# First attention of a two-layer mixer: how the side work of PE is dealt over the steps

## The chip, the cores and the metric

The kernel is one program on 1 core of a Trainium2 chip. The metric is the device time of that core in microseconds (us). TensorE is called PE, VectorE DVE, ScalarE ACT, GpSimd POOL, and SP issues most of the DMAs. All arithmetic is in float32; large products are made of three matmuls on operands that are split in a high and a low part.

## The reference

The program is a chain of blocks on a sequence of 512 tokens of width 1024. The change touches the attention of the first block, which runs in each of its two layers:

```python
h = rmsnorm(x, ln1_g[i]) @ w_in[i]
(fq, fk, fv, ff, dq, dk, dv, c_q, c_kv, k_r) = jnp.split(h, split_points, axis=-1)
o_fox  = fox_group(fq, fk, fv, ff, fgate_b[i])           # 4 heads of 64, causal, forget-gate bias
o_diff = diff_group(dq, dk, dv, ..., lam_init)           # 4 heads: softmax 1 - lam * softmax 2, values of 128, norm
o_mla  = mla_group(c_q, c_kv, k_r, ..., w_uq, w_ukv)     # 4 heads: q, k, v from a latent of 256 and of 128, with rope
x = x + jnp.concatenate([o_fox, o_diff, o_mla], axis=-1) @ w_o[i]
up = causal_dwconv(rmsnorm(x, ln2_g[i]) @ w_up[i], conv_w[i], conv_b[i])
x = x + (jax.nn.silu(up[..., :D_FF]) * up[..., D_FF:]) @ w_down[i]
```

Every softmax runs over the keys up to the query's own block of 128 (`fox_group` is causal inside it, the others use a mask of chunks of 64). After the two layers come an mLSTM mixer and a windowed attention, which the change leaves alone.

## The kernel before, in words

Activations lie transposed, a feature tile of 128 on the partitions and the 512 tokens along the free dimension. The attention of a layer is one loop over steps `s` = 0 to 67, written out on PE, ACT and DVE alike. Units 0 to 63 are the score blocks of 128 queries: `unit1(u)` gives the kind, the query block `i` and the head. Units 0 to 15 are the first group, in pairs of heads (n = 0, 1), units 16 to 47 the second (n = 2 to 5), of which an even and the following odd unit share one output, and units 48 to 63 the latent one. A unit of query block `i` has 128 x (i + 1) keys, so the work of a step grows with `i`, which is 0 to 3 over each eight steps.

In step `s` PE computes the scores of unit `s` (L762, L765) into bank `s % 3`, transposes the weights of unit `s - 3` (L778), multiplies those of unit `s - 4` with the values (`chain`, L593), and then does its filling, `fill1(s)`. DVE adds the bias and takes the maximum of the scores (L2074), mixes the two softmaxes of the second group (L2083, L2085, L2088), copies every other transposed block (L2103), scales the output (L2112) and then does `follow1(s)`. ACT computes the exponential (L1442), copies the other transposed blocks (L1451), and then does its own `follow1(s)`, which ends with splitting a weight unit into its high part (L1224), if `splits` names one for the step; POOL makes the low part (L2582). Between the splits POOL has the `scale_diff` operations (L2617), whose order is written out. Split weights have three slots: a unit can be split only when PE is through with the unit three back, and a load by SP waits for the split five units back.

The filling is the work that the softmax does not need at once:

- `tile_part`: K tiles ("k") and Q tiles ("q") of the next pairs of heads. A piece ("k", k0, kn) is kn of the 8 parts of the sum, three matmuls of 512 columns each (L563). Behind a whole K tile ACT writes its high half by 4 operations (L1323) and DVE its low half by 4 (L2002); behind a Q tile 2 and 2 (L1319, L1997). `LOW_STEPS` says in which step DVE does the low half.
- `value_tile`: one of four value tiles of 24 matmuls of 256 columns (L563), copied out by ACT.
- in steps 37 to 45 the latent parts: "mv" (values) and "mk" (keys), which ACT alone copies out (L1390, L1406), and "mq" (queries), of which ACT copies a part (L1401) and DVE turns the rest by three operations (L2041, L2043, L2047); and `turn_out`, which transposes the finished outputs of two heads (L685). ACT (L1366, L1369) and DVE (L2017, L2020) split these into `hH` and `hLo`.
- `out_part`: a piece of the output product with `w_o` (L563), which DVE adds to `x` (L2027); 12 matmuls in part 0, 6 in parts 1 and 2.

All filling uses banks 6 and 7 of the eight. Before PE writes a bank, `claim` makes it wait for the engine that reads the last result in it. Behind the last score, in step 64 and after the loop, the last outputs are transposed and part 2 follows.

## Time and profile before

| | us |
|---|---|
| median of 3 runs | 2560.44 (2558.16 to 2563.48) |
| the profiled execution | 2555.06 |
| its span in the profile | 2553.0 |
| PE busy | 2472.5 |
| DVE busy | 1222.8 |
| ACT busy | 987.8 |
| POOL busy | 978.5 |

A profile row of the timeline gives the start in us from the span's start, the duration in us, the engine, the line, the operation, what it writes and reads, how many instructions of that kind were merged, and in brackets how long the engine had been idle before it and whom it waited for. A matmul is pipelined: its duration is its latency, and the distance between two starts is what it costs. A step begins with the row of L762 in bank `s % 3`. In the first layer step 0 starts at 73.01 us, in the second at 735.27 us.

### The profile page before, as it was taken

The page shows a single profiled execution, that of the slowest core. Times are in us where ns is not written, and L with a number is a line of the kernel's source. Part 1 is how long each engine was busy: PE and PEld are TensorE (multiplying, and loading weights), DVE is VectorE, ACT ScalarE, POOL GpSimd, SP SyncE. Part 2 cuts the span into 40 slices and gives each one's busy share as a digit, 9 for nine tenths or more (in the row PEclk, how much of TensorE's full clock was granted, in tenths as well). Part 3 has the DMA queues.
Part 4 walks back from the last instruction along what each step waited for, and adds up shares of the span by engine and source line. Part 5 has one row for each costly group of instructions (what it writes and reads, how often), then busy time and mean ns, then how long its engine had stood idle before and what let it go on. Part 6 is the DMA issues. An engine that isn't in the chain of part 4 may idle for free.

```text
span 2553.0 us, 32345 instructions
## 1 busy us (share of the span) xinstructions
PE 2472.5 (97%) x12450; PEld 2013.9 (79%) x12450; DVE 1222.8 (48%) x2205; ACT 987.8 (39%) x1731; POOL 978.5 (38%) x512
## 2 busy tenths in 40 slices
PE   9998999999999899999999999999999999899998
PEld 6886788888788678888888778778787778887766
DVE  4356589530235747984116431622251252556663
ACT  5455344432345635444333313131222322455552
POOL 3322356764432225567663223222222323322231
PEclk9999999999999999999999999999999999999999
DMA  4211245322321114532331111112111111111000
GB/s 176 74 46 62 95 157 190 99 95 97 114 75 54 47 65 147 192 131 95 114 110 66 50 42 53 56 33 66 58 56 35 50 58 42 55 65 31 29 25 34
DMA packets 54584, 200.48 MB, mean 79 GB/s; under 512 B 6176, under 2 KB 6176, under 8 KB 53664
## 3 DMA queue, kind: packets, MB, share of 16 engines
q1 hardware_dynamic: 52272, 189.27, 21.9%
q10 hardware_dynamic: 2160, 9.15, 1.0%
q8 instruction: 100, 1.64, 0.3%
q14 instruction: 52, 0.43, 0.1%
HBM read 196.29 MB, written 2.10 MB: 78 GB/s over the span
## 4 chain that ended last, share of the span: by engine, by line
PE 77%; DVE 15%; ACT 3%; issue 2%; POOL 2%; DVEq 0%; ACTq 0%; POOLq 0%
PE ps L871 25%; PE ps L543 18%; PE ps L563 16%; PE ps L593 10%; DVE arena L1938 7%; DVE arena L2131 1%; PE ps L762 1%; DVE arena L2128 1%; DVE norm_sq L1902 1%; PE ps L1184 1%; POOL norm_acc L2595 1%; POOL wl L2582 1%; PE ps L778 1%; DVE hl L1914 1%; PE ps L988 1%
## 5 line engine op out<-in xcount | busy, mean ns | idle before, releaser
L2582 POOL TENSOR_TENSOR wl<-wring,wh 128x1024 fp32r<-128x1024 f32 (+1 forms) x305 | 770.5, 2526 | 1245.7 <-ACT wh L1224 1234.2
L1224 ACT ACTIVATE wh<-wring 128x1024 fp32r<-128x1024 f32 (+1 forms) x305 | 317.2, 1043 | 544.3 <-PE ps L871 307.9
L543 PE MATMUL ps<-hh,wh 128*128 128x512 f32 x768 | 300.0, 391 | 10.0 <-DVE hl L1914 5.1
L543 PE MATMUL ps<-hh,wl 128*128 128x512 f32 x768 | 299.0, 389 | 0.0
L543 PE MATMUL ps<-hl,wh 128*128 128x512 f32 x768 | 298.9, 389 | 0.0
L593 PE MATMUL ps<-arena 128*128 128x512 f32 (+2 forms) x912 | 265.2, 427 | 15.8 <-ACT arena L1451 5.8
L593 PEld LDWEIGHTS ps<-arena 128*128 128x128 f32 x912 | 141.5, 191 | 101.0 <-issue 77.4
L563 PE MATMUL ps<-hh,wh 128*128 128x512 f32 (+1 forms) x472 | 202.4, 429 | 5.0 <-DVE hl L2563 2.4
L563 PE MATMUL ps<-hh,wl 128*128 128x512 f32 (+1 forms) x472 | 189.1, 401 | 0.0
L563 PE MATMUL ps<-hl,wh 128*128 128x512 f32 (+1 forms) x472 | 188.7, 400 | 0.0
L1938 DVE CUSTOM_DVE_ANT_0 arena<-arena 128x1024 f32<-128x1024 f32 x96 | 182.6, 1902 | 8.6 <-DVE arena L2131 0.3
L543 PEld LDWEIGHTS ps<-hh,wh 128*128 128x128 f32 x768 | 144.1, 188 | 44.6 <-DVE hl L1914 5.2
L543 PEld LDWEIGHTS ps<-hh,wl 128*128 128x128 f32 x768 | 144.1, 188 | 30.1
L543 PEld LDWEIGHTS ps<-hl,wh 128*128 128x128 f32 x768 | 144.2, 188 | 28.7
L871 PE MATMUL ps<-hh,wh 128*128 128x512 f32 x368 | 144.3, 392 | 0.0
L871 PE MATMUL ps<-hl,wh 128*128 128x512 f32 x368 | 144.3, 392 | 0.0
L871 PE MATMUL ps<-hh,wl 128*128 128x512 f32 x368 | 143.1, 389 | 0.0
L543 PE MATMUL ps<-gu_h,wh 128*128 128x512 f32 x352 | 137.1, 390 | 0.0
L543 PE MATMUL ps<-gu_h,wl 128*128 128x512 f32 x352 | 136.9, 389 | 0.0
L543 PE MATMUL ps<-gu_l,wh 128*128 128x512 f32 x352 | 136.9, 389 | 0.0
L1442 ACT ACTIVATE arena<-arena,st 128x128 f32<-128x128 f32 (+3 forms) x128 | 71.8, 561 | 155.0 <-DVE st L2074 154.2
L2074 DVE CUSTOM_DVE_ANT_0 arena<-ps,arena 128x128 f32<-128x128 f32 (+3 forms) x128 | 62.5, 488 | 122.7 <-PE ps L765 63.8
(342 smaller groups left out, 5229.8 us busy)
## 6 DMA issues: line engine op xcount, KB each, us to landing
wring<-wts SPq DMA_DIRECT2D x290, 512.0 KB, 3.3
arena<-wts SPq DMA_DIRECT2D x48, 512.0 KB, 4.1
wring<-wts SPq DMA_DIRECT2D x16, 384.0 KB, 3.0
xL<-xt SPq DMA_DIRECT2D x4, 512.0 KB, 5.5
arena<-tab SPq DMA_DIRECT2D x1, 2048.0 KB, 16.0
arena<-cv ACTq DMA_DIRECT2D x2, 1024.0 KB, 4.9
arena<-tab ACTq DMA_DIRECT2D x1, 2048.0 KB, 7.8
out_t<-xL ACTq DMA_DIRECT2D x8, 256.0 KB, 2.0
```

The costliest lines, as they stand in the source:

```text
L543: mm = nc.tensor.matmul(o[0], a, b, start=start and k == first and j == 0, stop=stop and k == last and j == 2)
L563: mm = nc.tensor.matmul(dst, a, b, start=start and x == 0 and i == 0 and j == 0, stop=stop and x == len(us) - 1 and i == kn - 1 and j == 2)
L593: last = nc.tensor.matmul(dst, a, b, start=start and i == 0, stop=stop and i == len(pairs) - 1)
L762: last = nc.tensor.matmul(ps[:, s % 3, 0:ke], a, b, start=x == 0, stop=x == len(bs) - 1 and kind != "fox")
L778: last = nc.tensor.transpose(ps[:, 3 + tb, 128 * j:128 * j + 128], sbuf[:, u % 4, 128 * j:128 * j + 128], idn)
L871: mm = nc.tensor.matmul(dst, a, b, start=x == 0 and i == 0 and j == 0, stop=x == len(us) - 1 and i == kn - 1 and j == 2)
L988: nc.tensor.matmul(c, mlv[:, s, cols], cut(dense(s, 0), TC), start=s == 0, stop=s == 1)
L1224: nc.scalar.activation(wh[:, sn % SPLIT_SLOTS, :kn * w], raw(u)[:, :kn * w], ACT.Copy).then_inc(act_done, tick("act", ("hi", u)))
L1442: nc.scalar.activation(sbuf[:, s % 4, 0:ke], sbuf[:, s % 4, 0:ke], ACT.Exp, scale=-1.0, bias=mx1[:, s % 16:s % 16 + 1], accum_out=rs1[:, s ...
L1938: V.tensor_tensor_reduce(out=ada_dump, in0=raw(u), in1=crow[:, j, :], scale=1.0, scalar=0.0, op0=ALU.mult, op1=ALU.add, accum_out=modv[:, ...
L2074: V.tensor_tensor_reduce(out=sbuf[:, s % 4, 0:ke], in0=ps[:, s % 3, 0:ke], in1=bias, scale=-scale, scalar=3e38, op0=ALU.add, op1=ALU.min, ...
L2582: G.tensor_tensor(wl[:, sn % SPLIT_SLOTS, :kn * w], raw(u)[:, :kn * w], wh[:, sn % SPLIT_SLOTS, :kn * w].bitcast(F32), ALU.subtract).then_inc(
```

## The change

The filling of steps 0 to 31 is dealt evenly. A piece now has the number of its tile as well, (x, n, k0, kn); a value tile can be done in parts; two K tiles and two Q tiles come first in each 16 steps, and the value tiles come last, where they stood between the first and the second K tile before. The order of the weight units, of the splits on ACT and POOL and of `LOW_STEPS` follows. Steps 32 to 36 keep their pieces as `LAST_PIECES`.

In steps 37 to 47 the latent parts and the transposed outputs alternate: "mv" in steps 37 and 39, "mk" in 37, 39, 41 and 43, `turn_out` in 38 and 40, "mq" in 41, 42, 44 and 46. The first piece of output part 0 moves from step 46 to 45. Pieces 6 and 7 of output part 1 move from steps 61 and 62 to steps 64 and 65, into banks 2 and 1, ahead of the `turn_out` of step 64. `fill1` and `follow1` therefore run in every step up to 67.

```diff
-            if n in (0, 1, 3):
-                add(("v", l, (n + 1) // 2), "w_in", l, 0, KT, [((FV, DV, DV + 256)[(n + 1) // 2], 256)])
+            if n in (0, 2, 4):
+                add(("v", l, n // 2), "w_in", l, 0, KT, [((FV, DV, DV + 256)[n // 2], 256)])
+        add(("ukv", l), "w_ukv", l, 0, 1, [(128 * h, 64) for h in range(4)] + [(128 * h + 64, 64) for h in range(4)])
         add(("uq", l), "w_uq", l, 0, 2, [c for h in range(4)
                                          for c in ((96 * h, 96), (96 * h + 80, 16), (96 * h + 64, 16))])
-        add(("ukv", l), "w_ukv", l, 0, 1, [(128 * h, 64) for h in range(4)] + [(128 * h + 64, 64) for h in range(4)])
...
-PIECES = [[("k", 0, 3)], [("k", 3, 3)], [("k", 6, 2), ("q", 0, 1)], [("q", 1, 4)], [("q", 5, 3)],
-          [("v", 0, 0)], [("v", 1, 0)], [("v", 2, 0)], [("v", 3, 0)],
-          [("k", 0, 3)], [("k", 3, 3)], [("k", 6, 2), ("q", 0, 1)], [("q", 1, 3)], [("q", 4, 2)], [("q", 6, 2)], []]
-LOW_STEPS = {3: ("k", 1), 5: ("q", 1), 12: ("k", 2), 14: ("q", 2), 19: ("k", 3), 21: ("q", 3), 28: ("k", 4),
-             30: ("q", 4), 35: ("k", 5), 36: ("q", 5)}
-OUT0_STEPS = (46, 47, 48, 49, 50, 51, 52, 54)
+PIECES = [[("k", 1, 0, 3)], [("k", 1, 3, 3)], [("k", 1, 6, 2), ("q", 1, 0, 1)], [("q", 1, 1, 3)], [("q", 1, 4, 3)],
+          [("q", 1, 7, 1), ("k", 2, 0, 2)], [("k", 2, 2, 3)], [("k", 2, 5, 3)], [("q", 2, 0, 3)], [("q", 2, 3, 3)],
+          [("q", 2, 6, 2), ("v", 0, 0, 2)], [("v", 0, 2, 6)], [("v", 1, 0, 6)], [("v", 1, 6, 2), ("v", 2, 0, 4)],
+          [("v", 2, 4, 4), ("v", 3, 0, 2)], [("v", 3, 2, 6)]]
+LAST_PIECES = [[("k", 1, 0, 3)], [("k", 1, 3, 3)], [("k", 1, 6, 2), ("q", 1, 0, 1)], [("q", 1, 1, 4)], [("q", 1, 5, 3)]]
+LOW_STEPS = {3: ("k", 1), 6: ("q", 1), 8: ("k", 2), 11: ("q", 2), 19: ("k", 3), 22: ("q", 3), 24: ("k", 4),
+             27: ("q", 4), 35: ("k", 5), 36: ("q", 5)}
+MV_STEPS = {37: 0, 39: 1}
+MK_STEPS = {37: 2, 39: 3, 41: 0, 43: 1}
+MK_BANKS = {2: 7, 3: 7, 0: 7, 1: 6}
+MQ_STEPS = {41: 0, 42: 1, 44: 2, 46: 3}
+MQ_BANKS = (6, 7, 6, 6)
+OT_STEPS = {38: (0, 1), 40: (2, 3), 53: (4, 5)}
+OUT0_STEPS = {45: (0, 7), 47: (1, 7), 48: (2, 6), 49: (3, 7), 50: (4, 6), 51: (5, 7), 52: (6, 6), 54: (7, 6)}
+OUT1_STEPS = {55: (0, 7), 56: (1, 6), 57: (2, 7), 58: (3, 6), 59: (4, 7), 60: (5, 6), 64: (6, 2), 65: (7, 1)}
+
+
+def pieces_of(s):
+
+    return PIECES[s % 16] if s < 32 else LAST_PIECES[s - 32] if s < 37 else ()
...
-                def value_tile(j, t, b):
+                def value_tile(j, t, b, k0=0, kn=KT):
 
                     us = views(("v", l, j))
-                    claim([b], "act", "v", l, j, t)
-                    product(ps[:, b, 0:256], lat_toks(t), us, ("v", l, j, t),
-                            *([("used", x[0]) for x in us] if t == NT - 1 else []))
+                    if k0 == 0:
+                        claim([b], "act", "v", l, j, t)
+                    part = []
+                    for u, o, n, v in us:
+                        x, y = max(o, k0), min(o + n, k0 + kn)
+                        if x < y:
+                            part.append((u, x, y - x, [r[:, x - o:y - o, :] for r in v]))
+                    end = k0 + kn == KT
+                    product(ps[:, b, 0:256], lat_toks(t), part, *([("v", l, j, t)] if end else []),
+                            *([("used", x[0]) for x in us] if end and t == NT - 1 else []), start=k0 == 0, stop=end)
...
-                    pieces = PIECES[s % 16] if s < 32 else PIECES[s - 32] if s < 37 else ()
-                    for x, c, m in pieces:
+                    for x, n, c, m in pieces_of(s):
                         if x == "v":
-                            value_tile(1 + s // 16, c, 6 + c % 2)
+                            value_tile(1 + s // 16, n, 6 + n % 2, c, m)
                         else:
-                            tile_part(x, 2 * (s // 16) + (1 if s % 16 < 9 else 2), 6 if x == "k" else 7, c, m)
-                    if s == 37:
-                        pe.wait_ge(dve_done, at("dve", "h", ("ckv", l), 0))
+                            tile_part(x, 2 * (s // 16) + n, 6 if x == "k" else 7, c, m)
+                    if s in MV_STEPS:
+                        x = MV_STEPS[s]
+                        if x == 0:
+                            pe.wait_ge(dve_done, at("dve", "h", ("ckv", l), 0))
                         (n, _, w), = plain(("ukv", l))
-                        for t in range(NT):
-                            if t % 2 == 0:
-                                claim([6 + t // 2], "act", "mv", l, t // 2)
-                            chain(ps[:, 6 + t // 2, 256 * (t % 2):256 * (t % 2) + 256],
+                        claim([6], "act", "mv", l, x)
+                        for t in (2 * x, 2 * x + 1):
+                            chain(ps[:, 6, 256 * (t % 2):256 * (t % 2) + 256],
                                   [(cn[:, 2, 128 * t:128 * t + 128], w[:, 0, 256:512])], ("mv", l, t))
-                    elif s in (38, 39):
-                        for x in range(2):
-                            turn_out(2 * (s - 38) + x, 6 + x, 0, 1, 2, 3)
-                    elif 40 <= s < 44:
-                        r = s - 40
+                    if s in OT_STEPS:
+                        for x, k in enumerate(OT_STEPS[s]):
+                            turn_out(k, 6 + x, 0, 1, 2, 3)
+                    if s in MQ_STEPS:
+                        r = MQ_STEPS[s]
+                        b = MQ_BANKS[r]
                         if r == 0:
                             for m in range(2):
                                 pe.wait_ge(dve_done, at("dve", "h", ("cq", l), m))
                         (n, _, w), = plain(("uq", l))
-                        claim([7 - r % 2], "dve", "mq", l, r)
-                        chain(ps[:, 7 - r % 2, :], [(w[:, k, 128 * r:128 * r + 128], cn[:, k, :]) for k in range(2)],
+                        claim([b], "dve", "mq", l, r)
+                        chain(ps[:, b, :], [(w[:, k, 128 * r:128 * r + 128], cn[:, k, :]) for k in range(2)],
                               ("mq", l, r), *([("used", n)] if r == 3 else []))
-                    elif s in (44, 45):
+                    if s in MK_STEPS:
+                        h = MK_STEPS[s]
+                        b = MK_BANKS[h]
                         (n, _, w), = plain(("ukv", l))
-                        for h in (2 * s - 88, 2 * s - 87):
-                            claim([7 - h % 2], "act", "mk", l, h)
-                            chain(ps[0:64, 7 - h % 2, :], [(w[:, 0, 64 * h:64 * h + 64], cn[:, 2, :])], ("mk", l, h),
-                                  *([("used", n)] if h == 3 else []))
-                    elif s in OUT0_STEPS:
-                        out_part(0, OUT0_STEPS.index(s), 6 + s % 2)
-                    elif s == 53:
-                        for x in range(2):
-                            turn_out(4 + x, 6 + x, 0, 1, 2, 3)
-                    elif 55 <= s < 63:
+                        claim([b], "act", "mk", l, h)
+                        chain(ps[0:64, b, :], [(w[:, 0, 64 * h:64 * h + 64], cn[:, 2, :])], ("mk", l, h),
+                              *([("used", n)] if h == 1 else []))
+                    if s in OUT0_STEPS:
+                        out_part(0, *OUT0_STEPS[s])
+                    if s in OUT1_STEPS:
                         if s == 55:
                             pe.wait_ge(dve_done, at("dve", "ot", l, 5, 1))
-                        out_part(1, s - 55, 6 + s % 2)
+                        out_part(1, *OUT1_STEPS[s])
...
-                splits = {0: ("q", l, 1), 1: ("v", l, 1, first), 3: ("v", l, 1, second), 5: ("k", l, 2),
-                          9: ("q", l, 2), 10: ("k", l, 3), 12: ("q", l, 3), 15: ("v", l, 2, first),
-                          19: ("v", l, 2, second), 21: ("k", l, 4), 25: ("q", l, 4), 26: ("k", l, 5),
-                          28: ("q", l, 5), 31: ("wo", l, 0, 0), 35: ("wo", l, 0, 1), 37: ("wo", l, 0, 2),
-                          48: ("wo", l, 0, 3), 50: ("wo", l, 1, 0), 52: ("wo", l, 1, 1), 55: ("wo", l, 2, 0),
-                          59: ("wo", l, 2, 1)}
+                splits = {0: ("q", l, 1), 1: ("k", l, 2), 4: ("q", l, 2), 6: ("v", l, 1, first), 9: ("v", l, 1, second),
+                          12: ("k", l, 3), 16: ("q", l, 3), 17: ("k", l, 4), 20: ("q", l, 4), 22: ("v", l, 2, first),
+                          25: ("v", l, 2, second), 28: ("k", l, 5), 32: ("q", l, 5), 33: ("wo", l, 0, 0),
+                          35: ("wo", l, 0, 1), 37: ("wo", l, 0, 2), 48: ("wo", l, 0, 3), 50: ("wo", l, 1, 0),
+                          52: ("wo", l, 1, 1), 55: ("wo", l, 2, 0), 59: ("wo", l, 2, 1)}
...
-                    if s < nu:
-                        follow1(s)
-                    elif s == nu:
+                    follow1(s)
+                    if s == nu:
                         low_out(6, 6, 0, 1, 2)
                         low_out(7, 7, 0, 1, 2)
...
-                split(("k", l, 1))
-                split(("q", l, 1))
-                split(("v", l, 1))
-                for n in (2, 3):
+                for n in (1, 2):
                     split(("k", l, n))
                     split(("q", l, n))
+                split(("v", l, 1))
+                split(("k", l, 3))
+                split(("q", l, 3))
+                split(("k", l, 4))
+                split(("q", l, 4))
                 split(("v", l, 2))
-                split(("k", l, 4))
                 scale_diff(0)
-                split(("q", l, 4))
+                scale_diff(1)
                 split(("k", l, 5))
-                scale_diff(1)
+                scale_diff(2)
                 split(("q", l, 5))
-                scale_diff(2)
                 split(("wo", l, 0, 0))
```

The other two engines' `follow1` read the same tables: ACT and DVE do their part of each piece in the step in which PE does it, apart from `LOW_STEPS`.

## Rows read from the trace of the kernel before

**Rows 1.** The page: busy us of each engine.

```profile
PE 2472.5 (97%) x12450; PEld 2013.9 (79%) x12450; DVE 1222.8 (48%) x2205; ACT 987.8 (39%) x1731; POOL 978.5 (38%) x512
```

**Rows 2.** Stretches, layer 1: us; busy of PE, PEld, DVE, ACT, POOL; PEclk; DMA; GB/s.

```profile
73.00:125.95 52.95, 51.59 (x339) 46.84 (x337) 21.07 (x72) 27.31 (x60) 16.75 (x7) 1.00 0.22 70
125.95:131.90 5.95, 5.19 (x21) 4.19 (x22) 1.97 (x9) 2.63 (x6) 2.38 (x1) 0.71 0.03 5
131.90:175.23 43.33, 43.33 (x278) 38.91 (x276) 25.71 (x76) 24.17 (x61) 12.32 (x7) 1.00 0.17 55
175.23:183.24 8.01, 5.60 (x21) 4.23 (x20) 5.83 (x15) 5.54 (x16) 1.74 (x3) 0.79 0.20 65
...
195.38:229.94 34.56, 26.84 (x115) 16.03 (x114) 26.18 (x69) 19.80 (x52) 7.13 (x6) 1.00 0.12 38
...
280.56:291.73 11.17, 8.56 (x66) 7.21 (x64) 5.60 (x18) 3.68 (x9) 0.00 (x0) 1.00 0.01 1
291.73:303.00 11.27, 11.27 (x43) 9.18 (x44) 4.15 (x6) 5.00 (x8) 7.13 (x5) 0.85 0.68 234
```

**Rows 3.** The same stretch of steps 37 to 46 in the second layer.

```profile
857.62:892.18 34.56, 26.85 (x115) 16.04 (x114) 26.19 (x69) 19.79 (x52) 7.14 (x6) 1.00 0.12 38
```

**Rows 4.** PE's waits, 73 to 292 us: total, times, longest.

```profile
PE ps L762 <- DVE qs L1997: 3.2, 2, 1.8
PE ps L593 <- ACT arena L1451: 2.9, 3, 1.5
...
PE ps L593 <- DVE arena L2103: 1.4, 1, 1.4
```

**Rows 5.** PE's timeline: matmuls of the filling, 512 and 256 columns.

```profile
74.22 0.39 PE L563 MATMUL ps<-hh,wl 128*128 128x512 f32 x1
74.45 0.40 PE L563 MATMUL ps<-hh,wh 128*128 128x512 f32 x1
...
88.42 0.28 PE L563 MATMUL ps<-wh,hl 128*128 128x256 f32 x1
88.54 0.28 PE L563 MATMUL ps<-wh,hh 128*128 128x256 f32 x1
```

**Rows 6.** Stretches: steps 14 and 17.

```profile
120.32:123.05 2.73, 2.73 (x18) 2.39 (x16) 1.61 (x9) 1.80 (x5) 1.05 (x1) 1.00 0.24 35
131.90:135.28 3.38, 3.38 (x23) 2.99 (x21) 1.35 (x5) 0.49 (x2) 0.00 (x0) 1.00 0.46 151
```

**Rows 7.** PE's timeline: starts of steps 16 and 32, filling of step 16.

```profile
125.95 0.33 PE L762 MATMUL ps<-kh,qs 128*128 128x128 f32 x1 [1.34 <-DVE qs L1997]
...
129.54 0.63 PE L563 MATMUL ps<-hh,wh 128*128 128x512 f32 x1
...
178.97 0.33 PE L762 MATMUL ps<-kh,qs 128*128 128x128 f32 x1 [1.82 <-DVE qs L1997]
```

**Rows 8.** Instructions of L2085; timelines of DVE and POOL, step 36; page, L1224.

```profile
L2085 DVE SCALAR_TENSOR_TENSOR st<-st x32: 219/219/1981, 136.3 to 897.0; 128x1 f32<-128x1 f32 x32
...
194.50 1.97 DVE L2085 SCALAR_TENSOR_TENSOR st<-st 128x1 f32<-128x1 f32 x1
...
194.08 2.38 POOL L2582 TENSOR_TENSOR wl<-wring,wh 128x1024 fp32r<-128x1024 f32 x1 [0.34 <-ACT wh L1224]
...
L1224 ACT ACTIVATE wh<-wring 128x1024 fp32r<-128x1024 f32 (+1 forms) x305 | 317.2, 1043 | 544.3 <-PE ps L871 307.9
```

**Rows 9.** Timelines of PE and DVE, steps 40 to 43.

```profile
208.49 1.95 PE L593 MATMUL ps<-arena,wring 128*128 128x512 f32 x4 [2.38 <-DVE hl L2017]
...
217.22 1.16 PE L593 MATMUL ps<-arena 128*128 128x128 f32 x8 [1.55 <-ACT arena L1451]
...
210.48 0.70 DVE L2041 TENSOR_TENSOR arena<-ps,arena 32x512 f32<-32x512 f32 x1 [0.29 <-PE ps L593]
```

**Rows 10.** Steps 61 and 62 as a stretch; PE's timeline behind the last score.

```profile
sum 6.50, PE 6.50 PEld 4.92 DVE 3.86 ACT 2.01 POOL 0.00; mean PE 3.25 PEld 2.46 DVE 1.93 ACT 1.00 POOL 0.00
...
291.73 0.52 PE L563 MATMUL ps<-hh,wh 128*128 128x512 f32 x1 [0.76 <-DVE hl L2020]
```

More of the change, by code:

```diff
@@ new lines, in follow1 @@
+                def follow1(s):
+                    for x, n, c, m in pieces_of(s):
+                        if c + m == KT:
+                            if x == "v":
+                                evacuate_v(1 + s // 16, n, 6 + n % 2)
+                            else:
+                                high_tile(x, 2 * (s // 16) + n, 6 if x == "k" else 7)
+                    if s in MV_STEPS:
+                        x = MV_STEPS[s]
+                        act.wait_ge(pe_done, at("pe", "pv", l, 31))
+                        act.wait_ge(pe_done, at("pe", "mv", l, 2 * x + 1))
+                        nc.scalar.activation(mv[:, 2 * x:2 * x + 2, :],
+                                             ps[:, 6, :].rearrange("p (t c) -> p t c", t=2), ACT.Copy).then_inc(
+                            act_done, tick("act", ("mv", l, x)))
+                    if s in OT_STEPS:
+                        for x, k in enumerate(OT_STEPS[s]):
+                            high_out(k, 6 + x, 0, 1, 2, 3)
+                    if s in MQ_STEPS:
+                        r = MQ_STEPS[s]
@@ L2034, in follow1 @@
                         low_tile(x, n, 6 if x == "k" else 7)
-                    if 40 <= s < 44:
-                        r = s - 40
-                        b = 7 - r % 2
+                    if s in OT_STEPS:
+                        for x, k in enumerate(OT_STEPS[s]):
+                            low_out(k, 6 + x, 0, 1, 2, 3)
+                    if s in MQ_STEPS:
+                        r = MQ_STEPS[s]
+                        b = MQ_BANKS[r]
                         dve.wait_ge(pe_done, at("pe", "mq", l, r))
@@ L2048, in follow1 @@
                             dve_done, tick("dve", ("mq", l, r)))
-                    elif s in (38, 39):
-                        for x in range(2):
-                            low_out(2 * (s - 38) + x, 6 + x, 0, 1, 2, 3)
-                    elif s in OUT0_STEPS:
-                        add_out(0, OUT0_STEPS.index(s), 6 + s % 2)
-                    elif s == 53:
-                        for x in range(2):
-                            low_out(4 + x, 6 + x, 0, 1, 2, 3)
-                    elif 55 <= s < 63:
-                        add_out(1, s - 55, 6 + s % 2)
+                    if s in OUT0_STEPS:
+                        add_out(0, *OUT0_STEPS[s])
+                    if s in OUT1_STEPS:
+                        add_out(1, *OUT1_STEPS[s])
                 nu = 64
```

37 lines of the change are left out of this document (8 added, 29 removed).

## The prediction

> **What bounds the kernel now.** I read the engine totals first. PE is busy 2472.5 us of a span of 2553.0 us, every other engine under half of it [rows 1], and the change removes no matmul. So the only time to be won is time in which PE waits, or runs at the lower of its two clocks. Next I cut the first attention of the first layer into stretches at the starts of its score matmuls. In a "waited" stretch PE's busy time falls short of the stretch; in a "slow" one the granted clock falls under 1.00 [rows 2]. PE idles 1.36 (to 125.95) + 0.76 + 2.41 + 7.72 + 2.61 = 14.9 us in the five that have any to speak of. The clock is 1.2 instead of 2.4 GHz in three places: 0.71 over 5.95 us, 0.79 over 8.01 us and 0.85 over 11.27 us. Work lost there is (1 - 0.71) x 5.95 = 1.73, 0.21 x 8.01 = 1.68 and 0.15 x 11.27 = 1.69 us. The second layer repeats the longest of them to 0.01 us [rows 3], so I work out one layer and double it. The two layers hold 2 x (14.9 + 5.1) = 40 us: this is the ceiling.
>
> Then the list of waits tells who ends the idle times: L1997 (the low half of a query tile) 3.2 us, L1451 (ScalarE's copy of transposed weights) 2.9 us, L2103 (VectorE's copy) 1.4 us [rows 4]; L2017 (the low half of a transposed output) ends 2.38 us at once [rows 9].
>
> **Part 1: the filling dealt evenly over 16 steps.** The unit prices come from successive starts: a 512-column matmul of the filling takes 0.23 us, a 256-column one 0.12 us [rows 5]. Before, steps 0 to 15 held 9, 9, 9, 12, 9 matmuls of 0.23 us, then four value tiles of 24 x 0.12 = 2.88 us, then 9, 9, 9, 9, 6, 6 and nothing. The sum is 96 x 0.23 + 96 x 0.12 = 33.6 us; the new list has the same matmuls, 9 x 0.23 = 2.07 us or 18 x 0.12 = 2.16 us in each step. PE's work is unchanged.
>
> What goes are two waits per layer. Step 15 has no filling and step 16 needs the query tile finished at step 14: the row at 125.95 says that PE idled 1.34 us for L1997. Then the clock fell, the filling's matmuls took 0.63 us instead of 0.40 (129.54) [rows 7], and step 16 took 5.95 us [rows 2]. Step 17, the same shape and filling, took 3.38 [rows 6]. The excess is 2.57 us, and with the 1.34 us before it 3.9 us. The same happens at step 32: 1.82 us idle ahead of it [rows 7], 2.41 in all, and 1.68 us of clock: 4.1 us. In the new order the query tile of pair 2 is complete in step 10 and its low half runs in step 11, five steps before its reader; that of pair 4 runs in step 27. What ends last in step 15 is then a value tile, whose first reader comes in step 20. I take both waits and both drops of the clock as gone: 3.9 + 4.1 = 8.0 us, less 0.5 us for small waits that the steps with K tiles may show. The bounds are 8.0 and 4.6 us (the waits go, 1.34 + 0.76 + 2.41, but the clock falls somewhere else).
>
> Costs of this part. Each value tile is now cut in two, with no more matmuls and no more signals. In steps 5 to 8 the filling falls from 2.88 to 2.07 us; whether the softmax chain is then late can be read from step 14, which has the longest keys (512) and only 1.38 us of filling: PE was busy all its 2.73 us [rows 6]. So 0, up to 13 us (a rival below). The ring of three split weights is next: both units of a value tile are freed only by the last piece, in steps 15 and 31. Then ScalarE's split (1.04 us) in step 16 and GpSimd's 2.38 us [rows 8] have to be done before step 18's third piece, about 7.7 us later (2 x 2.9 + 1.9). With a softmax exponential (0.6 us on average) and the start of the step ahead of it on ScalarE the tile is ready after some 4.7 us. That leaves 3 us of slack: 0. SP's loads go in the new order of the units; a load waits for the split five units back, which is steps old, and `ukv` and `uq` only swap: 0. Part 1 gives 7.5 us a layer.
>
> **A resource to weigh.** L2085 on VectorE, 0.22 us in the median, took 1.97 us from 194.50, while GpSimd ran a 2.38 us split from 194.08, and ended with it [rows 8]. The copy L2103 behind it then ended PE's 1.42 us wait in step 37. Splits issued by ScalarE in odd steps meet this operation in the next even step. The operation runs in steps 18 to 48 only. Before there were six such splits (19, 21, 25, 31, 35, 37), now there are five (17, 25, 33, 35, 37). So this costs nothing new, and the 1.42 us in step 37 stays, since step 35's split stays. (The Trainium skill, "SBUF — State Buffer", section "Who interferes with whom", says that a VectorE instruction with two SBUF inputs and a GpSimd one that reads SBUF exclude each other for the whole instruction; this trace agrees, 1.97 against 0.22 us. If the stalls landed on a full VectorE they would cost 2 us each by it; it alone would not turn the sign.)
>
> **Part 2: steps 37 to 47.** Before, PE idled 7.72 us from 195.38 to 229.94 with VectorE busy 26.18 us of 34.56 [rows 2]. The order held all value parts, then four transposed outputs, then the latent queries one a step, then the keys. The largest wait, 2.38 us at 208.49, has the first query part waiting for the low halves of outputs 2 and 3 (L2017), whose banks it reuses; 1.55 us at 217.22 come from VectorE and ScalarE being late, as VectorE works through three query operations of 0.7 us in each of four steps [rows 9]. Now key and value parts, which only ScalarE reads, lie between the outputs, and the queries stand in 41, 42, 44 and 46. I followed the new order through the three engines with these durations. Step 37: 1.42 stays. Step 39: 0.8 for L1451 stays, 0.5 for the low half of output 0 stays (it now holds up the value part). Step 40: 0.3. Step 41: 0.5 for a copy by VectorE, and 1.2 for the low half of output 2, the old 2.38 us halved: it still comes some 2.9 us behind its transposes, as ScalarE has the norm of step 39 and an exponential first, but 1.7 us of scores and value products of step 41 now lie between. Step 43: 0.1. Step 44: 0.65, since the third query part takes the bank of key part 1, whose copy stands behind a softmax exponential. Sum 5.5 against 7.7: 2.2 us, of which I take 1.7. The bounds are 0 (every wait finds a successor, as VectorE has the same work in the same stretch) and 6.3 (all but the 1.42 go).
>
> **Part 3: two output pieces behind the last score.** Pieces 6 and 7 of output part 1, 6 x 0.23 = 1.38 us each, leave steps 61 and 62 and stand behind the value products of steps 64 and 65. Steps 61 and 62 took 3.25 us each with a piece, so 1.87 without. So everything from the last score on comes 2.76 us earlier. VectorE was busy 3.86 us in two such steps with the additions of two pieces, 0.69 us each, which leaves (3.86 - 1.38) / 2 = 1.24 us of work in a step of 1.87 [rows 10] and the chain keeps pace. From the start of step 63 to the last part PE waited 2.61 us [rows 2], in five waits of 0.24, 0.53, 0.54, 0.54 and, before the last part, 0.76 us [rows 10]. Piece 6 delays the transposes of outputs 6 and 7 by 1.38 us, and with them the low halves (L2020) that stood ahead of the copy for step 66: the 0.53 us wait goes, the last three waits stay, as product, scaling, transposing, splitting and the first matmul of the last part wait for each other whatever stands before. Piece 7 takes the place of 0.5 us of waiting and moves the rest by 0.9. In sum 1.4 us of 2.76 is hidden (bounds 0 and 2.6).
> The third fall of the clock, 1.69 us, comes with the last part's first matmuls, from 291.73 [rows 2]. The thin stretch ahead of it, the 7 us up to 291.73, shrinks to the last 4.2 us, as piece 7 has full matmuls. I count half of it, 0.8 us, between 0 and 1.7.
>
> **Sum.** One layer 7.5 + 1.7 + 1.4 + 0.8 = 11.4 us, two 23 us. The profiled execution took 2555.06 us (the span 2553.0 and 2.06 around it), so it would take 2532. It lies 5.4 us under the median of 2560.44; from the median I predict 2537.5.
>
> **Rivals.**
> A, the clock follows the waits: steps 38 and 40 hold only transposes beside the softmax, so from step 40 to the first query part in 41 PE has some 4.7 us of thin work with 2 us of waiting in it, about what stood before each fall. Against it: 195.38 to 229.94 has clock 1.00 with 7.72 us idle [rows 2]. One fall there and one left in the tail give back 2 x (1.7 + 0.8), and part 2 at nothing 2 x 1.7 more: 2537.5 + 8.4 = 2546. (The Trainium skill, "TensorE: Matmul & The Clock Gate", section "A second HAM failure mode: psum-queue depth-cycling", says that frequent small idle times between groups of matmuls make the clock oscillate. That would put a fall already in the old steps 37 to 47; the trace has none there.) Chance 0.22.
> B, the long-key steps miss their filling: four steps of each 16 with 2.88 - 2.07 = 0.81 us less cover, all waited for, 0.81 x 4 x 2 x 2 = 13 us: 2550. Against it is step 14. Chance 0.08.
> C, slower: the key and query tiles now land in steps 7, 8 and 10, 11, beside the longest softmax, and VectorE, which has 4 x 0.7 us for a key tile and 2 x 0.7 for a query tile (the size of L2041, [rows 9]) in one lump ahead of the next step's softmax, sends PE waiting for each. Eight tiles a layer are 4 x 2.8 + 4 x 1.4 = 17 us, two layers 34, against 23 gained: 2560.4 + 11 = 2571. It decides once such a lump is longer than the two steps (5 us and more) by which PE runs ahead. Against it: VectorE was busy 25.71 us of 43.33 in steps 17 to 30 [rows 2]. Chance 0.04.
> D, the change does more: nearly all waits of part 2 go too, and the third clock fall with them: 23 + 2 x (4.6 + 0.9) = 34: 2526. Chance 0.14.
> E, it does nothing, as another wait or the ring of weights takes each one's place: 2560. Chance 0.04. The forecast itself holds 0.48.
>
> **Range.** The forecast's own range is 2531 to 2544. With A, most of B, and half of D: 2527 to 2551. Faster than before by over 0.2% (5 us; what a measurement here can tell from no change) are the forecast, A, B, D: 0.92; same 0.04; slower 0.04.
>
> **What would show it.** No idle time ahead of steps 16 and 32 and clock 1.00 there; steps 16 and 32 near 3.4 and 2.7 us; the first query part (step 41) waiting about 1 us for L2017's successor in place of 2.38; steps 37 to 46, which hold the same parts in both orders, near 32.9 us instead of 34.56; from the start of step 63 to the last part's first matmul 12.5 us instead of 11.17, since step 63 starts 2.8 us earlier. The prediction is wrong if PE waits in steps 5 to 12, if the clock falls between steps 38 and 43, or if the weight ring's split ends a wait in step 18 or 34.

## The result, and the profile after

The changed kernel took 2538.09 us in the median of 4 runs (2534.49 to 2539.47), beside 2559.3 us for the kernel before. The ratio is 0.9917, with an interval of 0.9902 to 0.9932. So it is faster, by 21 us, and 0.6 us off the forecast of 2537.5. Timed again later beside its own runs of the kernel before, it took 2538.33 us (2534.25 to 2540.8), with a ratio of 0.991 [0.9893, 0.9926] (experiment 9).

The profiled execution took 2534.49 us. Its page starts like this, to be read against [rows 1]:

```profile
span 2532.8 us, 32353 instructions
...
PE 2466.3 (97%) x12450; PEld 2009.7 (79%) x12450; DVE 1217.8 (48%) x2205; ACT 986.0 (39%) x1731; POOL 977.3 (39%) x512
```

The number of matmuls is the same. PE is busy 6 us less, most of it the clock (5 us, see below), and idle 14 us less: (2553.0 - 2472.5) - (2532.8 - 2466.3) = 14.0 us.

The same cut into stretches as in [rows 2], of the first layer. The columns are window, length, busy time and count of PE, PEld, DVE, ACT and POOL, granted clock, DMA share and GB/s. The rows are step 0 to 15, step 16, steps 17 to 30, steps 31 and 32, steps 37 to 46, step 63 to the last part, and the last part's first 11 us:

```profile
73.08:124.78 51.70, 51.67 (x339) 46.89 (x338) 22.31 (x76) 26.54 (x60) 14.35 (x6) 1.00 0.19 62
124.78:128.05 3.27, 3.27 (x22) 2.90 (x21) 0.66 (x4) 2.20 (x5) 0.66 (x1) 1.00 0.02 5
128.05:169.60 41.55, 41.22 (x259) 36.75 (x258) 25.33 (x81) 25.78 (x64) 14.93 (x8) 1.00 0.20 66
169.60:175.28 5.68, 5.68 (x40) 5.21 (x39) 2.84 (x10) 3.01 (x12) 0.43 (x1) 1.00 0.10 36
187.43:219.42 31.99, 26.54 (x116) 15.86 (x114) 23.80 (x66) 18.55 (x49) 6.68 (x6) 1.00 0.05 17
267.68:281.01 13.33, 11.25 (x78) 9.50 (x78) 6.60 (x21) 4.86 (x12) 0.00 (x0) 1.00 0.00 1
281.01:292.30 11.29, 11.29 (x51) 9.35 (x52) 4.88 (x8) 5.17 (x8) 8.69 (x5) 1.00 0.69 234
```

PE's busy time equals the length in step 16 and in steps 31 and 32: both waits of part 1 are gone, and the clock is 1.00 where it was 0.71 and 0.79. One wait of 0.33 us is new, in step 21, in both layers; it is the only one over 0.05 us in steps 0 to 36:

```profile
141.69 0.49 PE L607 MATMUL ps<-arena 128*128 128x128 f32 x2 [0.33 <-DVE arena L2115]
```

In steps 37 to 46 PE still idles 5.4 us, where it idled 7.7. These are the waits, in PE's timeline:

```profile
189.38 0.49 PE L607 MATMUL ps<-arena 128*128 128x128 f32 x2 [1.44 <-DVE arena L2115]
190.91 1.04 PE L607 MATMUL ps<-arena,wring 128*64 128x512 f32 x2 [0.18 <-DVE qs L2012]
195.17 0.71 PE L607 MATMUL ps<-arena 128*128 128x128 f32 x4 [0.79 <-ACT arena L1466]
196.47 1.10 PE L607 MATMUL ps<-wring,arena 128*128 128x256 f32 x4 [0.59 <-DVE hl L2035]
200.97 0.94 PE L607 MATMUL ps<-arena 128*128 128x128 f32 x6 [0.63 <-DVE arena L2115]
202.73 2.96 PE L607 MATMUL ps<-arena,wring 128*128 128x512 f32 x6 [0.82 <-DVE hl L2032]
212.31 1.95 PE L607 MATMUL ps<-arena,wring 128*128 128x512 f32 x4 [0.99 <-ACT arena L1424]
```

Behind the last score, to be read against [rows 10]; the L577 rows from 271.38 are piece 6, those from 274.75 are piece 7:

```profile
270.49 1.08 PE L607 MATMUL ps<-arena 128*128 128x64 f32 x8 [0.24 <-DVE st L2108]
271.38 0.48 PE L577 MATMUL ps<-hh,wh 128*128 128x512 f32 x1
...
273.94 1.00 PE L607 MATMUL ps<-arena 128*128 128x64 f32 x8
274.75 0.48 PE L577 MATMUL ps<-hh,wh 128*128 128x512 f32 x1
...
276.66 1.00 PE L607 MATMUL ps<-arena 128*128 128x64 f32 x8
278.20 1.08 PE L607 MATMUL ps<-arena 128*128 128x64 f32 x8 [0.54 <-DVE arena L2124]
279.82 0.43 PE L706 MATMUL ps<-prmt,arena 128*128 128x128 f32 x2 [0.54 <-DVE arena L2124]
281.01 0.51 PE L577 MATMUL ps<-hh,wh 128*128 128x512 f32 x1 [0.76 <-DVE hl L2035]
```

Of the five waits, only the second (0.53 us) is gone. In the kernel before it was this one:

```profile
287.31 1.08 PE L593 MATMUL ps<-arena 128*128 128x64 f32 x8 [0.53 <-DVE st L2096]
```

Where the 20.2 us between the two spans went, start to start of score matmuls, layer 1 (layer 2 agrees to 0.06 us or better):

| steps | before | after | gain | of it not clock |
|---|---|---|---|---|
| 0 to 36 | 122.37 | 114.35 | 8.02 | 4.6 |
| 37 to 47 | 38.20 | 36.06 | 2.14 | 2.14 |
| 48 to 60 | 40.48 | 40.52 | 0 | 0 |
| 61 to the last part | 17.67 | 17.00 | 0.67 | 0.67 |

What is not clock, 2 x (4.6 + 2.14 + 0.67) = 14.8 us, I count as waits; PE's idle time fell by 14.0 us. What is left, 5.4 us, is clock. The granted clock agrees: before, up to the last part of layer 2, it was low for 3.41 us at six places, 20.5 us in all, and after for 3.4 + 6.8 = 10.2 us; half of the difference is 5.1 us. It is less than the 2 x (3.4 + 1.7) us that the three old places had cost, since the clock now fell in a new place, in the projections at the head of layer 2:

```profile
683.00:695.00 12.00, 11.14 (x42) 9.07 (x43) 0.69 (x1) 1.25 (x2) 6.75 (x4) 0.86 0.41 132
703.00:713.00 10.00, 10.00 (x23) 5.68 (x23) 4.17 (x6) 7.27 (x12) 3.54 (x3) 0.66 0.17 52
```

Layer 2's step 0 therefore started only 735.27 - 727.63 = 7.6 us earlier, though layer 1 had gained 8.02 + 2.14 + 0.67 and the 1.7 us of its last part, 12.5 in all.

### The profile page after: what moved, and what is told of

Read it like the earlier page. It is cut to its first block, busy times and chain, and to the rows that moved or that the text cites. A ratio compares the mean times of both kernels' runs of the same rounds, so it can differ in the third digit from the quotient of the medians.

```text
span 2532.8 us, 32353 instructions
## 1 busy us (share of the span) xinstructions
PE 2466.3 (97%) x12450; PEld 2009.7 (79%) x12450; DVE 1217.8 (48%) x2205; ACT 986.0 (39%) x1731; POOL 977.3 (39%) x512
## 4 chain that ended last, share of the span: by engine, by line
PE 78%; DVE 15%; ACT 3%; issue 2%; POOL 2%; DVEq 0%; ACTq 0%; POOLq 0%
PE ps L890 25%; PE ps L557 19%; PE ps L577 16%; PE ps L607 11%; DVE arena L1953 7%; PE ps L782 2%; DVE arena L2142 1%; DVE arena L2139 1%; DVE norm_sq L1917 1%; PE ps L1203 1%; PE ps L798 1%; POOL norm_acc L2606 1%; POOL wl L2593 1%; DVE hl L1929 1%; PE ps L1007 1%
## 5 line engine op out<-in xcount | busy, mean ns | idle before, releaser
L577 PE MATMUL ps<-hh,wh 128*128 128x512 f32 (+1 forms) x472 | 199.3, 422 | 5.0 <-DVE hl L2574 2.4
L577 PE MATMUL ps<-hh,wl 128*128 128x512 f32 (+1 forms) x472 | 186.6, 395 | 0.0
L577 PE MATMUL ps<-hl,wh 128*128 128x512 f32 (+1 forms) x472 | 185.9, 394 | 0.0
```

The source lines that it names most:

```text
L577: mm = nc.tensor.matmul(dst, a, b, start=start and x == 0 and i == 0 and j == 0, stop=stop and x == len(us) - 1 and i == kn - 1 and j == 2)
```

## The experiments

One table for the stretches, layer 1 / layer 2 where they differ by over 0.1 us; ratios stand with each experiment. Experiments 5 and 9 are those of "after" to 0.13 us; of 6, 7 and 8 the text names the one stretch that each changes.

| kernel | median | steps 0 to 36 | 37 to 47 | 61 to the last part |
|---|---|---|---|---|
| before | 2559 to 2562 | 122.37 | 38.20 | 17.67 |
| after | 2538.09 | 114.35 | 36.06 | 17.00 |
| 1: part 1 alone | 2547.63 | 114.35 | 39.52 / 39.70 | 17.85 / 18.66 |
| 2: parts 1 and 2 | 2541.66 | 114.38 | 36.09 | 17.87 / 18.69 |
| 3: part 3 alone | 2558.32 | 120.78 / 122.36 | 38.21 | 17.00 |
| 4: new order, old lumps | 2541.42 | 115.92 | 36.08 | 17.00 |
| 10: 6, 7 and 8 together | 2529.31 | 114.30 | 34.34 | 16.43 |

**1. Part 1 alone.** The kernel before with the new `PIECES`, `LAST_PIECES`, `LOW_STEPS`, the value tile in parts, and the new orders of units and splits; everything from step 37 on, and `ukv` behind `uq`, as before.

> Only part 1 of the change: the filling of steps 0 to 31 dealt evenly, steps 37 on as before. My theory (the low half of a query tile finished one step before its reader, and the clock that falls behind it) expects steps 0 to 36 of each layer to take 114.4 us as in the changed kernel instead of 122.4, so 16 us less, and the stretch of steps 37 to 46 at its old 34.56 us. The fall of the clock behind the last score (1.7 us a layer) should still be there, as the thin stretch ahead of it is the old one. So about 2543 us. The rival, that the clock behind the last score depends only on how its look falls on the stretch, expects it to be gone in one or both layers here too, 3.4 us less.

Measured: 2547.63 us (2546.3 to 2552.84) against 2560.71, ratio 0.9957 [0.9941, 0.9974]. Steps 0 to 36 have the full gain, 8.0 us in each layer. But in the profiled execution (span 2550.8), the slowest of the four, most of it is given back: the clock fell for 6.8 us in the head of each layer, then in steps 40 and 41 in both layers, and for 6.8 instead of 3.4 us behind the last score. It fell so by 0.014 of the span in sum, against 0.009 before. In the old steps 37 to 47 that costs 1.3 to 1.5 us; the fall, at 205.1 us, comes right behind the old wait of the first query part:

```profile
204.35 3.03 PE L600 MATMUL ps<-arena,wring 128*128 128x512 f32 x4 [2.38 <-DVE hl L2029]
...
203.00:210.00 7.00, 5.64 (x16) 3.25 (x16) 5.47 (x15) 2.71 (x11) 3.08 (x3) 0.76 0.00 1
285.00:295.00 10.00, 8.22 (x31) 6.42 (x31) 2.45 (x6) 2.07 (x4) 2.37 (x1) 0.66 0.49 159
```

Part 1 saves 16 us in its own steps; alone it is worth 13 in the medians (2547.63 us, where 2543 was expected). (A clock that falls and rises again is what the Trainium skill, "TensorE: Matmul & The Clock Gate", section "A second HAM failure mode: psum-queue depth-cycling", gives as the result of frequent short idle times between groups of matmuls. The prediction said that the trace of before has no such fall in steps 37 to 47; this run of the same steps does, in both layers, so the rule holds there in some executions.)

**2. Parts 1 and 2, without part 3.**

```diff
-              ... 60: (5, 6), 64: (6, 2), 65: (7, 1)}
+              ... 60: (5, 6), 61: (6, 7), 62: (7, 6)}
```

> Parts 1 and 2 without part 3: pieces 6 and 7 stand in steps 61 and 62 again. I expect steps 37 to 47 at 36.1 us (38.2 before), and from the start of step 61 to the first matmul of the last part 17.67 us (17.00 in the changed kernel), so 1.3 us more than the changed kernel in both layers. If part 3 is what removed the fall of the clock there, it comes back: another 3.4 us. About 2543 us with it, 2539 us without.

Measured: 2541.66 us (2537.23 to 2542.78), ratio 0.9927 [0.9911, 0.9942]. Steps 37 to 47 are those of the changed kernel to 0.03 us, without a fall in the stretch where experiment 1 has one. Behind the last score the clock fell for 6.8 us in both layers:

```profile
203.00:210.00 7.00, 5.53 (x28) 3.18 (x27) 4.96 (x14) 4.53 (x15) 2.63 (x3) 1.00 0.00 1
282.00:292.00 10.00, 8.23 (x30) 6.33 (x30) 2.46 (x6) 2.38 (x5) 2.37 (x1) 0.66 0.52 170
```

So part 2 is worth 2.1 us of waits a layer, and against the one profile of experiment 1 another 1.4 of clock.

**3. Part 3 alone**, on the kernel before: pieces 6 and 7 of output part 1 in steps 64 and 65, nothing else.

> Only part 3 on the kernel before: pieces 6 and 7 behind the last score. The clock theory (the full matmuls of piece 7 shorten the thin stretch) expects the fall behind the last score gone in both layers and 0.67 us a layer besides: 4.7 us less than before. The rival (the position of the look decides, and nothing moves ahead of that place in layer 1 of the kernel before) expects a fall in at least one of the two layers: 1.3 to 3 us less.

Measured, in 10 runs: 2558.32 us (2555.36 to 2563.37), ratio 0.9995 [0.9984, 1.0005]: nothing that can be told from zero. The stretch is 17.00 us as in the changed kernel, so the gain is 0.67 us a layer and does not depend on the other parts. The clock fell at the last part in layer 1 and not in layer 2, as the rival had it; the 4.7 us of the clock theory lie outside the interval. And step 16 of layer 1, the same instructions as in [rows 2] with the same wait before it, ran at full clock here:

```profile
126.00:132.00 6.00, 4.05 (x25) 3.45 (x26) 3.16 (x12) 2.64 (x6) 2.25 (x1) 1.00 0.01 3
290.00:296.00 6.00, 5.29 (x16) 4.19 (x17) 1.81 (x4) 1.88 (x4) 2.37 (x1) 0.72 0.71 238
952.00:958.00 6.00, 4.15 (x23) 3.34 (x22) 1.75 (x5) 1.50 (x4) 1.92 (x1) 1.00 0.23 64
```

**4. The order or the even sizes?** The changed kernel with its new order of tiles, but the old sizes of the pieces: whole value tiles, and nothing in steps 15 and 31.

```diff
-PIECES = [[("k", 1, 0, 3)], [("k", 1, 3, 3)], [("k", 1, 6, 2), ("q", 1, 0, 1)], [("q", 1, 1, 3)], [("q", 1, 4, 3)],
-          [("q", 1, 7, 1), ("k", 2, 0, 2)], [("k", 2, 2, 3)], [("k", 2, 5, 3)], [("q", 2, 0, 3)], [("q", 2, 3, 3)],
-          [("q", 2, 6, 2), ("v", 0, 0, 2)], [("v", 0, 2, 6)], [("v", 1, 0, 6)], [("v", 1, 6, 2), ("v", 2, 0, 4)],
-          [("v", 2, 4, 4), ("v", 3, 0, 2)], [("v", 3, 2, 6)]]
+PIECES = [[("k", 1, 0, 3)], [("k", 1, 3, 3)], [("k", 1, 6, 2), ("q", 1, 0, 1)], [("q", 1, 1, 4)], [("q", 1, 5, 3)],
+          [("k", 2, 0, 3)], [("k", 2, 3, 3)], [("k", 2, 6, 2), ("q", 2, 0, 1)], [("q", 2, 1, 3)], [("q", 2, 4, 2)],
+          [("q", 2, 6, 2)], [("v", 0, 0, 8)], [("v", 1, 0, 8)], [("v", 2, 0, 8)], [("v", 3, 0, 8)], []]
```

> The changed kernel with the new order (two K and two Q tiles, then the values) but the old sizes: 9, 9, 9, 12, 9, 9, 9, 9, 9, 6, 6 matmuls of 512 columns, four whole value tiles of 2.88 us, and an empty step 15 and 31. If what matters is that the query tile is done five steps before its reader, steps 16 and 32 have no wait and the kernel is within 2 us of the changed one. If the even sizes matter (the empty step leaves PE nothing while the softmax chain runs), PE waits in steps 15 and 31, by about the 0.6 to 1.5 us of the old step 31, and the clock falls behind it: 3 to 10 us more than the changed kernel.

Measured: 2541.42 us (2541.0 to 2545.91), ratio 0.9934 [0.9917, 0.9952]. Steps 0 to 36 take 115.92 us: the order alone saves 6.45 of the 8.02 us a layer. No wait for a query tile is left, and steps 15 (1.38 us) and 16 (3.90 us) run at full clock though step 15 is empty. What the even sizes add, 1.6 us, is mostly one other wait, in the value step 27, for ScalarE's copy of the transposed weights (in this kernel the lines stand one number lower):

```profile
126.44:127.82 1.38, 1.38 (x14) 1.30 (x12) 0.49 (x1) 0.39 (x1) 0.00 (x0) 1.00 0.00 0
127.82:131.72 3.90, 3.60 (x22) 3.00 (x22) 1.49 (x9) 2.64 (x6) 0.83 (x1) 1.00 0.02 4
160.49:165.98 5.49, 4.25 (x35) 4.05 (x34) 2.59 (x7) 3.22 (x8) 2.96 (x2) 1.00 0.24 83
162.12 1.16 PE L606 MATMUL ps<-arena 128*128 128x128 f32 x8 [1.24 <-ACT arena L1465]
```

The median is 3.3 us over the changed kernel's. That is the size that the second expectation gave, but not its mechanism: no wait in steps 15 and 31, no fall behind them.

**5. The changed kernel once more**, unedited, for the places where the clock falls.

> The changed kernel once more, nothing edited, for its clock. My theory after the first runs: where the clock falls depends on how the chip's looks lie against the start of the execution, which differs from run to run, so the step lengths free of falls repeat to 0.03 us while the falls lie elsewhere than at 684.8 and 705.3 us. The rival (the kernel's own order sets the falls) expects the same two places.

Measured: 2537.94 us (span 2536.2). The steps repeat to 0.08 us, and to 0.03 us where no fall lies in the stretch; the falls do not. Four windows: the head of layer 1, two in the head of layer 2, and the last part of layer 2. First the two of the result's profiled execution that are not shown above, then all four of this one:

```profile
52.00:62.00 10.00, 10.00 (x39) 6.58 (x38) 4.17 (x6) 7.92 (x13) 3.96 (x3) 1.00 0.23 67
932.00:944.00 12.00, 10.16 (x49) 8.29 (x48) 4.51 (x9) 5.28 (x9) 6.12 (x4) 1.00 0.62 191
```

```profile
52.00:62.00 10.00, 10.00 (x23) 5.69 (x23) 4.17 (x6) 7.14 (x12) 3.40 (x3) 0.66 0.18 55
683.00:695.00 12.00, 10.07 (x45) 8.00 (x44) 2.21 (x7) 4.15 (x6) 8.44 (x4) 1.00 0.41 132
703.00:713.00 10.00, 10.00 (x28) 5.88 (x28) 4.34 (x7) 8.03 (x13) 4.12 (x2) 0.83 0.16 52
932.00:944.00 12.00, 10.23 (x38) 8.04 (x38) 3.15 (x7) 3.29 (x7) 3.57 (x2) 0.72 0.55 177
```

The first fell from 1.00 to 0.66, the second rose from 0.86 to 1.00, the fourth fell from 1.00 to 0.72. Up to there the clock was low for 17.0 us here and for 10.2 us there, and half of the difference, 3.4 us, is what lies between the spans. So the kernel's order alone does not set the places. They are not arbitrary either: a third profile of the same kernel (experiment 9, on another chip than this one) has its falls at 53.8, 709.2 and 934.5 us, within 0.2 us of those here. What sets them is open; the "looks" of the expectation are not tested by any run.

**6. ScalarE's split of `wo` 0, 1 one step later**, to test the 1.44 us wait of step 37.

```diff
-                          35: ("wo", l, 0, 1), 37: ("wo", l, 0, 2), ...
+                          36: ("wo", l, 0, 1), 37: ("wo", l, 0, 2), ...
```

> The changed kernel with the split of the second output weight in ScalarE's step 36 instead of 35. My theory says that the 1.44 us wait of PE in step 37 comes from GpSimd's part of this split, which holds up VectorE's mixing operation (L2085's successor) in step 36 for some 1.8 us; then the wait shrinks to under 0.3 us and step 37 from 4.45 to about 3.1 us. The rival (VectorE is late from the four low-half operations of the key tile in step 35 anyway) expects the wait to stay over 1 us. The wait that follows in step 39 may take some of it back.

Measured: 2536.16 us in one run; steps 37 to 47 take 35.56 us, 0.5 less. In the changed kernel L2097 lasts as long as GpSimd's split:

```profile
186.56 1.99 DVE L2097 SCALAR_TENSOR_TENSOR st<-st 128x1 f32<-128x1 f32 x1
186.14 2.38 POOL L2593 TENSOR_TENSOR wl<-wring,wh 128x1024 fp32r<-128x1024 f32 x1 [0.34 <-ACT wh L1243]
```

Here it is short again, the 1.44 us wait is gone, and another has taken most of its place: the low half of query tile 5 stands between PE and bank 7.

```profile
187.56 0.22 DVE L2097 SCALAR_TENSOR_TENSOR st<-st 128x1 f32<-128x1 f32 x1
189.87 1.41 DVE L2012 TENSOR_TENSOR qs<-ps,qs 64x512 fp32r<-64x512 f32 x2 [1.31 <-ACT qs L1338]
191.42 1.04 PE L607 MATMUL ps<-arena,wring 128*64 128x512 f32 x2 [1.39 <-DVE qs L2012]
```

The mechanism is shown, its price was 0.5 us and not 1.4: step 37 went from 4.46 to 3.96 us, where 3.1 was expected, since VectorE itself now waits 1.31 us for ScalarE's high half of that tile. (The Trainium skill, "SBUF — State Buffer", section "Who interferes with whom", says that a VectorE instruction with two SBUF inputs contends with a GpSimd one that reads SBUF; the traces agree: 1.99 us beside the split, 0.22 without.)

**7. The third query part in bank 7**, whose last reader is not behind an exponential; the banks of output part 0 change with it.

```diff
-MQ_BANKS = (6, 7, 6, 6)
-OUT0_STEPS = {45: (0, 7), 47: (1, 7), 48: (2, 6), 49: (3, 7), 50: (4, 6), 51: (5, 7), 52: (6, 6), 54: (7, 6)}
+MQ_BANKS = (6, 7, 7, 7)
+OUT0_STEPS = {45: (0, 6), 47: (1, 6), 48: (2, 7), 49: (3, 6), 50: (4, 7), 51: (5, 6), 52: (6, 7), 54: (7, 6)}
```

> The changed kernel with the third and fourth latent query part and the output pieces in the other of the two banks. In the changed kernel the third query part (step 44) takes bank 6 and waits 0.99 us for ScalarE's copy of the key part of step 43. In bank 7 its last reader is VectorE's work on the query part of step 42. I expect that wait under 0.3 us and steps 37 to 47 together about 0.7 us shorter (36.06 now). The rival: VectorE is the bound there and gives the time back at the next wait, so 0 to 0.2 us.

Measured: 2535.73 us in one run; steps 37 to 47 take 34.83 us, 1.23 less, all of it in step 44 (1.88 us instead of 3.12), where 0.7 was expected. The third query part, now at 214.83, waits for nothing:

```profile
214.27 0.44 PE L782 MATMUL ps<-kh,qs 128*128 128x384 f32 x1
...
214.83 1.88 PE L607 MATMUL ps<-arena,wring 128*128 128x512 f32 x4
```

**8. Pieces 6 and 7 later still**, in steps 66 and 67, where the 0.54 us waits are.

```diff
-              ... 60: (5, 6), 64: (6, 2), 65: (7, 1)}
+              ... 60: (5, 6), 66: (6, 2), 67: (7, 7)}
```

> The changed kernel with pieces 6 and 7 behind the value products of steps 66 and 67 instead of 64 and 65 (piece 7 in bank 7). Each then stands ahead of a wait of 0.54 us, where now piece 6 hides one of 0.53 and piece 7 none. From the start of step 61 to the last part's first matmul (17.00 us) I expect 16.4 us: two waits of 0.54 hidden, the one of 0.53 (or part of it) back. The rival, that the chain of the last unit (product, scaling, transposes) sets the end and each piece in it delays it in full, expects 17.5 us or more.

Measured: 2533.05 us in one run; from step 61 to the last part 16.45 us, 0.55 less than after. Both 0.54 us waits are hidden, the 0.53 us one is back, and the last is 0.96 us where it was 0.76:

```profile
275.49 1.08 PE L607 MATMUL ps<-arena 128*128 128x64 f32 x8 [0.53 <-DVE st L2108]
...
277.85 1.00 PE L607 MATMUL ps<-arena 128*128 128x64 f32 x8
...
281.46 0.50 PE L577 MATMUL ps<-hh,wh 128*128 128x512 f32 x1 [0.96 <-DVE hl L2035]
```

**9 and 10. The changed kernel timed again, and beside it on the same chip the edits of 6, 7 and 8 together.**

> The changed kernel, timed again beside the next one on the same chip: 2538 us, give or take 2 for the places at which its clock falls.

> The changed kernel with the three edits that shortened it alone: the split in step 36 (0.48 us a layer), the other bank for the third and fourth query part (1.23 us) and pieces 6 and 7 behind steps 66 and 67 (0.55 us). If they add up, steps 37 to 47 take 36.06 - 1.71 = 34.35 us and the tail 16.45, the kernel 4.5 us less than the changed one, near 2533.5 us. If VectorE were the bound in steps 37 to 47, the first two would not add up: 35 us or more there.

Measured: 2538.33 us (2534.25 to 2540.8) and 2529.31 us (2527.37 to 2535.4), beside 2561.93 us for the kernel before. The ratios are 0.991 [0.9893, 0.9926] and 0.9881 [0.9865, 0.9897]. Both are faster than before; the two intervals still overlap by 0.0004, and the ranges of four runs each by 1.2 us. The steps leave no doubt, however: 37 to 47 take 34.34 us where 36.06 - 0.50 - 1.23 = 34.33 was to be had, and 16.43 us are left from step 61 on.

```profile
190.90:221.17 30.27, 26.05 (x115) 15.92 (x114) 22.06 (x63) 19.49 (x50) 7.95 (x6) 1.00 0.05 18
```

These waits are worth 2 x (1.72 + 0.57) = 4.6 us of the 9 us between the medians. The rest goes, as far as the two profiles tell, with the clock: no fall behind the last score in either layer, where experiment 9 has one of 6.8 us in layer 2. Experiment 8 had none there either, so none in four layers with the pieces in steps 66 and 67. That speaks for the edit, but so few profiles don't show it.

## Why the prediction was right, and where it was not

**The sum.** Forecast 23 us, of it 2 x (4.1 + 1.7 + 1.4) = 14.4 us of waits and 2 x (3.4 + 0.8) = 8.4 us of clock. Measured between the profiled executions: 14.8 us and 5.4 us. The waits are right in sum, since parts 1 and 2 gave 1.9 us more than forecast and part 3 gave 1.5 less; the clock gave 3 us less. Of the clock, the four falls at steps 16 and 32 went as forecast (6.8 us) and the tail gave 3.4 us for 1.6, but 5.1 us were lost at the head of layer 2, for which the forecast had nothing. The medians differ by 21.2 us in the same comparison, 1 more than the spans. So the forecast of 23 us was 1.8 too high. That it hit the time to 0.6 us is in part luck: errors of 1.9, 1.5 and 3 us partly cancel, and the kernel before was itself 1.1 us faster in this comparison than the 2560.44 that the forecast started from.

**Part 1: right, in mechanism and size.** 7.5 us a layer forecast, 8.0 measured. Waits and drops at steps 16 and 32 are gone as read; of the 0.5 us kept back for new waits, 0.33 us came, in step 21. (The lower bound's 1.34 + 0.76 + 2.41 is 4.5, not 4.6.) That the drops go with the waits fits all profiles: in the old order (before, experiment 3) the clock fell at seven of the eight steps 16 and 32, in the new one at none of forty. Steps 16 and 32 take 3.27 and 2.61 us (3.4 and 2.7 forecast). Experiment 4 adds what the prediction did not separate: the query tile's earlier place removes both waits, and evening the sizes, which gives the change its name, is 1.6 us of the 8. The ring of weights and the long-key steps (rival B) cost nothing: steps 0 to 15 have 0.03 us of idle time, and no wait stands in step 18 or 34. Nor did rival C's lumps.

**Part 2: right, place by place.** The walk through the new order gave eight waits with 5.5 us in sum, and there are seven with 5.44 us. That the sums agree better than the places is luck. Step 37 has 1.44 + 0.18 (1.42 forecast), step 39 has 0.79 + 0.59 (0.8 + 0.5), step 41 has 0.63 + 0.82 (0.5 + 1.2), step 44 has 0.99 (0.65); only the 0.3 of step 40 and the 0.1 of step 43 are missing. The gain was 2.14 us, where I took 1.7 out of caution. Experiment 7 shows that the last of them came from the choice of the bank. The test named for it came out at 31.99 us for steps 37 to 46 against 32.9: the fourth query part of step 46 now runs into step 47, so that stretch flatters the change by 0.4 us.

**Part 3: the step that failed is "In sum 1.4 us of 2.76 is hidden".** It is 0.67 us. The prediction's own terms give less than 1.4: two pieces of 1.38 us that hide 0.53 and 0.5 us of waiting hide 1.0. Piece 6 does remove the 0.53 us wait, and the last three waits stay, as written. But "piece 7 takes the place of 0.5 us of waiting" is wrong: there is no wait of its kind at 274.75. In the new tail the three waits of 0.54, 0.54 and 0.76 us all lie behind both pieces, so piece 7 delays the whole chain in full. From step 63 on it took 13.33 us, not 12.5. Experiment 8, with both pieces put where these waits are, gets another 0.55 us; experiment 3 shows that the part alone can't be told from nothing.

**The clock behind the last score: not decided by piece 7.** I counted half of 1.69 us. In the six layers profiled with the pieces in 61 and 62 (before, experiments 1 and 2) the clock fell every time, for 3.4 or 6.8 us. With them in 64 and 65 it fell in 9 layers of 14: in neither layer of the result's profile, in one of two in experiments 3, 5 and 9, in both in 4, 6 and 7. Half of the low time, the cost, is 2.8 us a layer in the mean of the six and 1.5 us in that of the 14. So about half went, as assumed, but of a larger loss than the 1.69 us of the one trace, and the layers are few and of several kernels: the part shifts the odds at most. That the fall follows from the length of the thin stretch ahead of it, as the prediction had it, is not shown.

**Rival A was half right.** The clock does fall in steps 40 and 41: in both layers of experiment 1, with the old order and its wait of 2.38 us, which is 0.82 us in the new one. With the new order it stayed at 1.00 there in every profile. So A named the right place and the wrong kernel. That a fall comes back elsewhere, which only the lower bound of part 1 allowed for, is what happened at the head of layer 2. My statement against A, that these steps had clock 1.00 with 7.72 us idle, rested on one execution. B to E are out.

## What to carry to other kernels

A wait on a tile is removed by producing the tile earlier, not by spreading the filler that sits beside its reader; look for the reader first. To hide a stall with side work, put the work where the chain's last waits are, for work ahead of them delays the chain in full. Price waits and clock separately: step lengths at full clock repeat to some hundredths of a us, while where the clock falls differs between executions of one kernel, so one trace shows what a fall costs and not whether it will be there.
